# Scattered gate transfers packed into fewer steps, weight loads queued ahead of expert-weight loads, other accumulation banks, a square-root table loaded early

## The chip, the cores and the metric

The kernel runs on one core of one Trainium2 chip. The metric is the time of one execution on the device in microseconds (us); lower is better. The engines are TensorE (PE, matrix products; PEld is its weight load), VectorE (DVE), ScalarE (ACT), GpSimd (POOL), and SyncE (SP), which here only issues transfers. Transfers go over 16 DMA engines.

## What is computed

One decoder layer on 512 tokens of width 2048: a projection, a convolution branch and a differential attention branch, a gated mix, then a layer norm, a product-key mixture of experts ("PEER"), a second layer norm and a gated per-layer embedding. The change lies in the experts' part, and in a helper of the norms:

```python
q = (xb @ w_q).reshape(TOKEN_BLOCK, PEER_HEADS, 2, PEER_HALF)
s = einsum('thcd,hcnd->thcn', q, sub_keys)
vals, idx = lax.top_k(s, PEER_TOPK)            # 8 heads x 16 picks of 128 x 128 experts
...
g = softmax(best)
h = gelu(einsum('td,thkd->thk', xb, u_tab[ids]))
y = einsum('thk,thkd->td', g * h, v_tab[ids])
```

A token has 8 x 16 = 128 picks (head h, pick k; n = 16 h + k in the kernel).

## The kernel before

Every matrix product is made in three matmuls from operands split into a high and a low part (whi, wlo of the weights; ahi, alo of the data), so a block of 8 x 128 x 128 weights costs 24 matmuls. All weights, the two expert tables among them, stream through one buffer of two units (`raw`), a unit being 1 MB or two blocks. SP loads a unit once both low parts of the unit that lay there are made (`load_unit`, L398), ACT makes the high part (`hi_part`, L993) as soon as the block four earlier is done on PE, and the low part is made by POOL (L554) or, from block DVE_LO of the fifth stage on, by DVE (L1520).

**First expert stage** (blocks B5 to B6, 256 blocks in 64 steps of `expert_step`): PE multiplies the inputs of the first 416 tokens with all 16384 rows of `u_tab`; units alternate between PSUM banks 0 and 1. ACT applies gelu and writes the results into `expert_spill` in DRAM (L1182 to L1184, semaphores `gelu_out`, `evac5`). The last 128 tokens are not computed densely: POOL gathers rows of `u_tab` with an indirect DMA, 160 rows in all (`gather_u`, L602; buffer `urows`, four deep, so that row n waits for the use of row n - 4), and DVE takes the dot product of each (`extra_dot` L1532 for the first 32 rows, whose other operand `x1e` is in SBUF; `dot` L1526 for the others, whose other operand `quad` is in PSUM). DVE's order is written out by hand: `expert_tile` (L1559) is one low part, a few gate sums, and in three of four steps one dot; 24 rows go with 32 blocks.

**Gates.** For the first 384 tokens, in three groups a of 128, a dense matrix of gates is needed in DRAM beside the gelus. DVE sums the gates of equal picks (`sum_gate` L1538, `sum_gates` L1554: 384 sums spread over SUM_BLOCKS of the steps), and POOL scatters each column with an indirect DMA, one "put" of 128 words (`put_gate` L572, L580). There are 3 x 128 = 384 puts. `put_gates(n)` (L591) issues those whose entry in PUT_ROW is n just behind the gather of row n, on the same queue. Before the first put of each head but the first (n % 16 == 0), POOL waits until all earlier puts of the same group a have landed (L579). The order is: groups 0 and 1 with heads alternating, 256 puts; then group 2, 128 puts, head after head. The third group's gates need a result of the first 40 rows (`extra_gates`, issued behind row 76; DVE's wait L1548).

**Second expert stage** (from B6, 16 groups of 8 units): for each group DVE forms the products gate x gelu, eight slices (`expert_weights` L1601: three instructions a slice, semaphore `w_ok`), from `hg`, which SP loads from `expert_spill` in pairs of slices into two slots (`load_hg` L473). PE multiplies them with `v_tab` (`value_group` L897; unit u in banks 0,1 if u is even, 2,3 if odd), and DVE adds the results into `res` (L1653). The first product slice k of a group waits for w_ok of that slice. Slices 0 and 1 of the two kinds of `xwhi` and `xwlo` overlay `urows` and `ahi`, so the first group's slices are formed after the last dot, the second's after PE's last block of the first stage (L1630).

**SP's order at the border of the stages** (L480 to L522) is an in-order queue. Behind the load numbered k = 6 of the last twelve of the first stage it waits for all 384 puts (`put`), then loads hg slices 0 to 3. Behind the waits on w_ok that free a slot come the next pairs: ahead of that, or behind it, the loads of the weights.

PE waits for `evac5` of the last unit before it starts the second stage (L915).

**Norms**: `norm_squares` (L1006) squares 8 or 16 slices on ACT for PE to sum and then takes the square root; it is called three times.

Of the kernel before, what the change touches and what calls it, by code (L numbers as in the profile page):

```python
# [18 lines left out]
P = 128  # L19
# [27 lines left out]
U5 = 128  # L47
# [44 lines left out]
PUTS = 3 * NP  # L92
PUT_ROW = [6 + 154 * j // PUTS for j in range(PUTS)]
SUM_BLOCKS = 204

# [10 lines left out]
def build(nc, ws, xT, pT, cpar, pvec, lamT, keysT, u_tab, v_tab, out):  # L106
# [6 lines left out]
    with ExitStack() as ctx:  # L113
# [163 lines left out]
        gone = small("gone", [P, TD // P, NP])  # L277
        same = small("same", [P, 2, NP])
        xsrc = small("xsrc", [P, 2, NP])
# [117 lines left out]
        def _(sp):  # L397
# [82 lines left out]
            for k in range(2 * (64 - POST)):  # L480
                load_unit(B5 // 2 + 2 * POST + k, k % 2)
                if k == 2:
                    sp.dma_start(pin[:], pT).then_inc(p_in, 16)
                if k == 6:

                    for a in range(TD // P):
                        sp.wait_ge(put[a], 16 * NP)

                    for s in range(2):
                        sp.wait_ge(gelu_out[s], 16 * 4)  # L490
                    for s in range(2):
                        load_hg(s, s)
                if k in (9, 10):

                    sp.wait_ge(w_ok, 2 * (k - 7) - 2)
                    load_hg(k - 7, k - 9)

            def group_loads(g, first=False, hg_pairs=4):

                for k in range(8):  # L500
                    if first and k in (0, 2):

                        for s in range(2):
                            sp.wait_ge(gelu_out[s], 16 * (6 if k == 0 else U5 // 2))
                    if first and k == 0:
                        for pair in range(2):

                            sp.wait_ge(w_ok, 6 + 2 * pair)
                            load_hg(4 + pair, pair)
                    load_unit(g * 8 + (B6 // 2 + k), k % 2)  # L510
                    if k % 2 == 1 and k // 2 < hg_pairs:

                        sp.wait_ge(w_ok, g * 8 + (8 + k + 1))
                        load_hg(sp.snap(g * 4 + (6 + k // 2)), k // 2 % 2)
# [18 lines left out]
        def _(pool):  # L533
# [38 lines left out]
            def put_gate(a, n):  # L572

                if n == 0:
                    pool.wait_ge(offs_ok, 1)
                    pool.wait_ge(zero_out, 16 * NK // 4)
                pool.wait_ge(sum_ok, (n // TOPK * 2 + a) * TOPK + n % TOPK + 1 if a < 2 else 2 * NP + n + 1)
                if n % TOPK == 0 and n:
# [12 lines left out]
            def put_gates(n):  # L591

                if n == 3 * NTG + RING:
                    extra_gates()
                for j in range(PUTS):
                    if PUT_ROW[j] == n:
                        if j < 2 * NP:
                            put_gate(j // TOPK % 2, j // (2 * TOPK) * TOPK + j % TOPK)
                        else:
                            put_gate(TU // P, j - 2 * NP)  # L600

# [33 lines left out]
        def _(pe):  # L635
# [261 lines left out]
            def value_group(g, q):  # L897

                for u in range(8):

                    pe.wait_ge(evac6, g * 8 + (u + 1))
                    for half in range(2):
                        b, s = g * 16 + (B6 + 2 * u + half), 2 * (u % 2) + half
                        pe.wait_ge(lo_done, b + 1)
                        for k in range(8):
                            if u == 0 and half == 0:

                                pe.wait_ge(w_ok, g * 8 + (k + 1))
                            t = slice(k * P, (k + 1) * P)
                            mm = three(ps[s][:, 0:TD], whi[:, s, t], wlo[:, s, t],  # L910
                                       xwhi[q][:, k], xwlo[q][:, k], k == 0, k == 7)
                        mm.then_inc(blk_done, 1)


            pe.wait_ge(evac5, 2 + U5)  # L915
            with pe.Fori(0, 8) as i:
# [75 lines left out]
        def _(act):  # L992
# [12 lines left out]

            def norm_squares(i, n, src):  # L1006
                for k in range(n):

# [254 lines left out]
        def _(dve):  # L1263
# [277 lines left out]
            def sum_gate(j):  # L1541

                if j < 2 * NP:
                    a, n = j // TOPK % 2, j // (2 * TOPK) * TOPK + j % TOPK
                else:
                    a, n = TU // P, j - 2 * NP
                if j == 2 * NP:
                    dve.wait_ge(xw_in, 16 * NJ)  # L1548
                here = slice(0, n // TOPK * TOPK + TOPK)
                dve.scalar_tensor_tensor(same[:, j % 2, here], gflat[:, a, here], gflat[:, a, n:n + 1], gone[:, a, here],  # L1550
                                         ALU.is_equal, ALU.mult, accum_out=gval[:, a, n:n + 1]
# [78 lines left out]
            dve.wait_ge(blk_done, B6)  # L1630
            dve.wait_ge(p_in, 16)
            dve.tensor_copy(phi[:], pin[:])
            dve.drain()
            dve.tensor_tensor(plo[:], pin[:], phi[:].bitcast(F32), ALU.subtract).then_inc(p_ok, 1)

            dve.wait_ge(hd_gelu, 1)
            dve.tensor_tensor(hd[:], hd[:], gd[:], ALU.mult)

            def add_values(g, q, first=False, last=False):
                for u in range(8):  # L1640
# [10 lines left out]
                    for n in range(2):  # L1651
                        r = res[:, 2 * u + n, 0:TD]
                        p = ps[2 * (u % 2) + n][:, 0:TD]  # L1653
                        if first:
# [5 lines left out]
                    if last:  # L1660
                        for n in range(2):
# [3 lines left out]
                            else:  # L1665
                                dve.tensor_tensor(msum2[:, 0:TD], msum2[:, 0:TD], res[:, 2 * u + n, 0:TD], ALU.add)
                    if first:
                        for n in range(max(0, 2 * (u - 3)), 2 * (u - 2) if 3 <= u < 7 else 0):
# [93 lines left out]
```

## Time and profile before

| | |
|---|---|
| median of 3 runs | 3819.95 us (3818.35 to 3825.75) |
| the profiled execution | 3826.09 us |
| its span, first to last instruction | 3824.3 us |
| mean granted clock of PE | 0.990 |
| PE busy | 3726.1 us (97%), 19672 matmuls |
| DVE busy | 2615.9 us (68%) |
| ACT busy | 1231.7 us (32%) |
| POOL busy | 1638.9 us (43%) |
| puts, L580 | 384, 446.5 us |

All times in a trace are us from the start of its span. L580 is line 580 of the kernel above; "out<-in" names what an instruction writes and reads; the brackets hold the idle time ahead of an instruction and what ended it; PEclk is the granted share of full clock. The first expert stage runs from about 1450 to 2499, the second from 2505 to 3572. DMA_INDIRECT on POOL is the issue of a gather (L608, L619) or of a put (L580), not the transfer. Some matmul records can be missing from a trace.

### The profile page before, as it was taken

The page shows a single profiled execution, that of the slowest core. Times are in us where ns is not written, and L with a number is a line of the kernel's source. Part 1 is how long each engine was busy: PE and PEld are TensorE (multiplying, and loading weights), DVE is VectorE, ACT ScalarE, POOL GpSimd, SP SyncE. Part 2 cuts the span into 40 slices and gives each one's busy share as a digit, 9 for nine tenths or more (in the row PEclk, how much of TensorE's full clock was granted, in tenths as well). Part 3 has the DMA queues.
Part 4 walks back from the last instruction along what each step waited for, and adds up shares of the span by engine and source line. Part 5 has one row for each costly group of instructions (what it writes and reads, how often), then busy time and mean ns, then how long its engine had stood idle before and what let it go on. Part 6 is the DMA issues. An engine that isn't in the chain of part 4 may idle for free.

```text
span 3824.3 us, 55313 instructions
## 1 busy us (share of the span) xinstructions
PE 3726.1 (97%) x19672; PEld 3394.2 (89%) x19672; DVE 2615.9 (68%) x4104; ACT 1231.7 (32%) x1538; POOL 1638.9 (43%) x1010
## 2 busy tenths in 40 slices
PE   8999999999999999998999999799999999999999
PEld 6888888877887789998999999799999999999777
DVE  3555555553412799877898887678888888888632
ACT  4444444442112423344433332222222222222442
POOL 4444444434444345588777766421212121212233
PEclk9999999999999999999999999899999999999999
DMA  5433443324433123598999989778777777776222
GB/s 186 131 130 130 129 130 130 129 97 140 148 132 115 66 88 137 191 341 319 381 377 376 358 331 333 277 308 319 295 299 296 303 300 300 293 309 259 101 105 80
DMA packets 185328, 848.02 MB, mean 222 GB/s; under 512 B 28912, under 2 KB 70064, under 8 KB 97840
## 3 DMA queue, kind: packets, MB, share of 16 engines
q1 hardware_dynamic: 99760, 507.23, 36.7%
q0 software_dynamic: 54016, 302.28, 20.4%
q10 hardware_dynamic: 31488, 37.76, 2.8%
q8 instruction: 28, 0.46, 0.0%
q14 instruction: 36, 0.29, 0.0%
HBM read 784.02 MB, written 63.11 MB: 222 GB/s over the span
## 4 chain that ended last, share of the span: by engine, by line
PE 75%; DVE 9%; POOL 7%; issue 3%; DMA 3%; ACT 2%; DVEq 1%; ACTq 0%; SPq 0%; POOLq 0%
PE bank L638 24%; PE bank L640 24%; PE bank L639 24%; POOL expert_spill L580 5%; POOL urows L608 2%; DVE hot L1469 1%; DMA raw<-ws 1%; PE quad L681 1%; DMA expert_spill<-gval,goff 1%; DVE sc L1332 1%; PE bank L700 1%; DVE pick L1472 1%; DVE topi L1433 0%; DVE topi L1426 0%; DVE s4b L1427 0%
## 5 line engine op out<-in xcount | busy, mean ns | idle before, releaser
L999 ACT ACTIVATE whi<-raw 128x1024 fp32r<-128x1024 f32 x784 | 822.5, 1059 | 2465.1 <-PE bank L640 1684.3
L638 PE MATMUL bank<-ahi,whi 128*128 128x352 f32 (+1 forms) x3968 | 1431.3, 361 | 66.9 <-DVE wlo L1523 22.0
L640 PE MATMUL bank<-ahi,wlo 128*128 128x352 f32 (+1 forms) x3968 | 1419.1, 358 | 0.0
L639 PE MATMUL bank<-alo,whi 128*128 128x352 f32 (+1 forms) x3968 | 1417.4, 357 | 0.0
L557 POOL TENSOR_TENSOR wlo<-raw,whi 128x1024 fp32r<-128x1024 f32 x316 | 789.5, 2502 | 1054.9 <-ACT whi L999 1026.4
L638 PEld LDWEIGHTS bank<-ahi,whi 128*128 128x128 f32 x3968 | 753.6, 190 | 165.1 <-DVE wlo L1523 46.4
L640 PEld LDWEIGHTS bank<-ahi,wlo 128*128 128x128 f32 x3968 | 751.9, 189 | 77.8
L639 PEld LDWEIGHTS bank<-alo,whi 128*128 128x128 f32 x3968 | 751.3, 189 | 72.5 <-issue 0.5
L638 PE MATMUL bank<-xwhi,whi 128*128 128x384 f32 x2048 | 684.9, 334 | 5.8 <-DVE xwlo L1610 5.8
L640 PE MATMUL bank<-xwhi,wlo 128*128 128x384 f32 x2048 | 684.6, 334 | 0.0
L639 PE MATMUL bank<-xwlo,whi 128*128 128x384 f32 x2048 | 684.6, 334 | 0.0
L1523 DVE TENSOR_TENSOR wlo<-raw,whi 128x1024 fp32r<-128x1024 f32 x472 | 575.1, 1220 | 97.3 <-ACT whi L999 95.0
L619 POOL DMA_INDIRECT vrows<-v_tab,idx x128 | 213.4, 1667 | 871.6 <-DVE yacc L1621 776.5
L580 POOL DMA_INDIRECT expert_spill<-gval,goff x384 | 446.5, 1163 | 156.1 <-issue 119.2
L638 PEld LDWEIGHTS bank<-xwhi,whi 128*128 128x128 f32 x2048 | 385.0, 188 | 6.4 <-issue 6.4
L639 PEld LDWEIGHTS bank<-xwlo,whi 128*128 128x128 f32 x2048 | 385.0, 188 | 0.0
L640 PEld LDWEIGHTS bank<-xwhi,wlo 128*128 128x128 f32 x2048 | 384.9, 188 | 0.0
L1529 DVE SCALAR_TENSOR_TENSOR urows<-urows,quad 128x2048 f32<-128x2048 f32 x128 | 292.2, 2283 | 44.6 <-DMA urows<-u_tab,idx 44.3
L1621 DVE SCALAR_TENSOR_TENSOR yacc<-vrows,hd,yacc 128x2048 f32<-128x2048 f32 x127 | 298.7, 2352 | 24.4 <-issue 21.5
L1332 DVE SCALAR_TENSOR_TENSOR sc<-glu,cur,sc 128x512 f32<-128x512 f32 x232 | 270.1, 1164 | 17.3
L1658 DVE TENSOR_TENSOR res<-res,bank 128x384 f32<-128x384 f32 x240 | 121.9, 549 | 81.0 <-PE bank L640 81.0
L1298 DVE RECIPROCAL rcp<-sums 128x2 f32<-128x2 f32 x32 | 5.3, 166 | 231.2 <-ACTq L1056 231.2
(218 smaller groups left out, 2555.9 us busy)
## 6 DMA issues: line engine op xcount, KB each, us to landing
raw<-ws SPq DMA_DIRECT2D x394, 1024.0 KB
hg<-expert_spill SPq DMA_DIRECT2D x64, 768.0 KB, 7.4
expert_spill<-zero SPq DMA_DIRECT2D x32, 768.0 KB, 7.9
expert_spill<-hst ACTq DMA_DIRECT2D x128, 192.0 KB
gate_spill<-gout ACTq DMA_DIRECT2D x32, 256.0 KB, 2.1
gl<-gate_spill SPq DMA_DIRECT2D x32, 256.0 KB, 2.7
expert_spill<-gval,goff POOLq DMA_INDIRECT x384
xin<-xT SPq DMA_DIRECT2D x8, 512.0 KB, 8.7
```

The source lines that it names most:

```text
L557: nc.gpsimd.tensor_tensor(wlo[:, s], raw[:, s // 2, s % 2], whi[:, s].bitcast(F32), ALU.subtract).then_inc(lo_done, 1)
L580: nc.gpsimd.indirect_dma_start(eg_flat, bass.IndirectOffsetOnAxis(ap=goff[:, a, n:n + 1], axis=0), gval[:, a, n:n + 1], None).then_inc(put ...
L619: nc.gpsimd.indirect_dma_start(vrows[:, n % RING], None, v_tab, bass.IndirectOffsetOnAxis(ap=idx[:, n:n + 1], axis=0)).then_inc(rows_in[n ...
L638: pe.matmul(ps_out, hi, xh, start=first, stop=False)
L639: pe.matmul(ps_out, hi, xl, start=False, stop=False)
L640: return pe.matmul(ps_out, lo, xh, start=False, stop=last)
L999: act.activation(whi[:, s], raw[:, s // 2, s % 2], ACT.Copy).then_inc(hi_done, 1)
L1332: dve.scalar_tensor_tensor(dst, glu[:, w:w + T], cur[:, w:w + 1], acc, ALU.mult, ALU.add)
L1523: dve.tensor_tensor(wlo[:, s], raw[:, s // 2, s % 2], whi[:, s].bitcast(F32), ALU.subtract).then_inc(lo_done, 1)
L1529: dve.scalar_tensor_tensor(urows[:, s], urows[:, s], 1.0, quad[:], ALU.mult, ALU.mult, accum_out=hd[:, bass.ds(n, 1)]).then_inc(rows_used, 1)
L1621: dve.scalar_tensor_tensor(yacc[:], vrows[:, s], w, yacc[:], ALU.mult, ALU.add).then_inc(rows_used, 1)
L1658: ad = dve.tensor_tensor(r, r, p, ALU.add)
```

## The change

1. The 384 puts are spread over rows 6 to 145 instead of 6 to 159, their sums over 184 blocks instead of 204.
2. Their order is a list, PUT_ORDER. Groups 0 and 1 alternate for heads 0 to 6; then come the heads (2,0), (0,7), (2,1), (1,7), and then (2,2) to (2,7). `same` gets a third buffer. The index of the put in the list is what POOL waits for in `sum_ok`.
3. SP: the loads of hg pairs 2 and 3 move from behind k = 9 and 10 to behind k = 10 and 11; in the first group of the second stage the loads of pairs 4 and 5 move from ahead of its first weight load to behind its first and its second.
4. PE: units of the second stage use the other pair of banks (even 2,3; odd 0,1), and the wait for `evac5` moves from ahead of the stage to ahead of unit 1.
5. ACT: `norm_squares` begins with a square root of one column into `std`.
6. DVE: the split of `pin` into phi and plo moves from ahead of the second stage to the end of its first group.

```diff
-PUT_ROW = [6 + 154 * j // PUTS for j in range(PUTS)]
-SUM_BLOCKS = 204
+PUT_ROW = [6 + 140 * j // PUTS for j in range(PUTS)]
+SUM_BLOCKS = 184
+PUT_HEADS = [(a, h) for h in range(7) for a in (0, 1)]
+PUT_HEADS += [(2, 0), (0, 7), (2, 1), (1, 7)] + [(2, h) for h in range(2, 8)]
+PUT_ORDER = [(a, h * TOPK + k) for a, h in PUT_HEADS for k in range(TOPK)]
+FIRST_EXTRA = PUT_ORDER.index((2, 0))
...
-        same = small("same", [P, 2, NP])
+        same = small("same", [P, 3, NP])
...
-                if k in (9, 10):
-                    sp.wait_ge(w_ok, 2 * (k - 7) - 2)
-                    load_hg(k - 7, k - 9)
+                if k in (10, 11):
+                    sp.wait_ge(w_ok, 2 * (k - 8) - 2)
+                    load_hg(k - 8, k - 10)
...
-                    if first and k == 0:
-                        for pair in range(2):
-                            sp.wait_ge(w_ok, 6 + 2 * pair)
-                            load_hg(4 + pair, pair)
                     load_unit(g * 8 + (B6 // 2 + k), k % 2)
+                    if first and k < 2:
+                        sp.wait_ge(w_ok, 6 + 2 * k)
+                        load_hg(4 + k, k)
...
-                pool.wait_ge(sum_ok, (n // TOPK * 2 + a) * TOPK + n % TOPK + 1 if a < 2 else 2 * NP + n + 1)
+                pool.wait_ge(sum_ok, PUT_ORDER.index((a, n)) + 1)
...
-                        if j < 2 * NP:
-                            put_gate(j // TOPK % 2, j // (2 * TOPK) * TOPK + j % TOPK)
-                        else:
-                            put_gate(TU // P, j - 2 * NP)
+                        put_gate(*PUT_ORDER[j])
...
+                        bank = 2 * ((u + 1) % 2) + half
+                        if u == 1 and half == 0:
+                            pe.wait_ge(evac5, 2 + U5)
...
-                            mm = three(ps[s][:, 0:TD], whi[:, s, t], wlo[:, s, t],
+                            mm = three(ps[bank][:, 0:TD], whi[:, s, t], wlo[:, s, t],
...
-            pe.wait_ge(evac5, 2 + U5)
             with pe.Fori(0, 8) as i:
...
             def norm_squares(i, n, src):
+                act.activation(std[:, 0:1], eps[:], ACT.Sqrt)
...
-                if j < 2 * NP:
-                    a, n = j // TOPK % 2, j // (2 * TOPK) * TOPK + j % TOPK
-                else:
-                    a, n = TU // P, j - 2 * NP
-                if j == 2 * NP:
+                a, n = PUT_ORDER[j]
+                if j == FIRST_EXTRA:
                     dve.wait_ge(xw_in, 16 * NJ)
...
-            dve.wait_ge(p_in, 16)
-            dve.tensor_copy(phi[:], pin[:])
-            dve.drain()
-            dve.tensor_tensor(plo[:], pin[:], phi[:].bitcast(F32), ALU.subtract).then_inc(p_ok, 1)
...
-                        p = ps[2 * (u % 2) + n][:, 0:TD]
+                        p = ps[2 * ((u + 1) % 2) + n][:, 0:TD]
...
+                    if first and u == 7:
+                        dve.wait_ge(p_in, 16)
+                        dve.tensor_copy(phi[:], pin[:])
+                        dve.drain()
+                        dve.tensor_tensor(plo[:], pin[:], phi[:].bitcast(F32), ALU.subtract).then_inc(p_ok, 1)
```

## Rows read from the trace of the kernel before

**Rows 1.** Busy time by stretch: PE, PEld, DVE, ACT, POOL, PEclk, DMA share, GB/s

```profile
1600.00:1700.00 100.00, 97.32 (x603) 96.53 (x602) 77.95 (x153) 48.95 (x53) 72.73 (x51) 1.00 0.85 326
1700.00:1800.00 100.00, 88.87 (x523) 86.61 (x522) 70.99 (x137) 40.47 (x44) 81.72 (x61) 0.97 0.89 313
1900.00:2000.00 100.00, 100.00 (x623) 100.00 (x622) 90.95 (x171) 33.72 (x42) 76.14 (x70) 1.00 0.99 379
...
2300.00:2400.00 100.00, 95.05 (x569) 93.92 (x568) 78.85 (x141) 26.33 (x34) 65.38 (x59) 0.97 0.88 325
2400.00:2460.00 60.00, 50.77 (x290) 49.32 (x289) 38.23 (x61) 11.78 (x15) 41.66 (x40) 0.94 0.82 295
```

**Rows 2.** Waits of PE, 2450 to 2520: total us, times, longest us

```profile
PE bank L638 <- ACT hst L1182: 19.1, 1, 19.1
PE bank L638 <- DVE xwlo L1610: 5.8, 1, 5.8
```

**Rows 3.** Busy time by stretch around the border, columns as in rows 1

```profile
2470.00:2480.00 10.00, 5.50 (x25) 5.51 (x26) 6.71 (x5) 4.71 (x6) 0.00 (x0) 0.62 0.53 189
...
2500.00:2510.00 10.00, 4.79 (x19) 4.82 (x20) 9.29 (x15) 2.92 (x5) 4.24 (x4) 0.66 1.00 393
```

**Rows 4.** SP's queue in order of time, start and us of each stretch

```profile
2401.81 28.87 SPq L403 DMA_DIRECT2D raw<-ws  x4
2463.28 0.89 SPq L475 DMA_DIRECT2D hg<-expert_spill  x2
2464.22 13.99 SPq L403 DMA_DIRECT2D raw<-ws  x3
2491.21 0.38 SPq L475 DMA_DIRECT2D hg<-expert_spill  x1
2491.64 0.47 SPq L403 DMA_DIRECT2D raw<-ws  x1
```

**Rows 5.** Timelines of POOL: one group-2 wait, row 145's gather, the last put

```profile
2244.39 0.97 POOL L580 DMA_INDIRECT expert_spill<-gval,goff  x1 [8.93 <-DMA expert_spill<-gval,goff]
...
2378.39 1.17 POOL L608 DMA_INDIRECT urows<-u_tab,idx  x1 [0.30 <-issue]
...
2459.59 0.97 POOL L580 DMA_INDIRECT expert_spill<-gval,goff  x1 [0.30 <-issue]
```

**Rows 6.** Timelines of DVE (L1606, L1610) and ACT (L1182) at the border

```profile
2487.84 0.56 DVE L1606 TENSOR_TENSOR wt<-hg 128x384 f32<-128x384 f32 x1 [0.30 <-issue]
...
2504.26 0.56 DVE L1610 TENSOR_TENSOR xwlo<-wt,xwhi 128x384 fp32r<-128x384 f32 x1
2504.32 0.44 ACT L1182 ACTIVATE hst<-bank 128x352 f32<-128x352 f32 x1
```

**Rows 7.** POOL's busy time with puts (L580) alone, by stretch

```profile
1626.00:1796.00 170.00, 104.11 (x70) 0.98 0.90 327
1796.00:2200.00 404.00, 219.02 (x203) 1.00 0.99 372
```

**Rows 8.** All engines from 1796 to 2200, columns as in rows 1

```profile
1796.00:2200.00 404.00, 401.07 (x2489) 400.78 (x2489) 354.60 (x666) 142.21 (x170) 310.66 (x288) 1.00 0.99 372
```

**Rows 9.** Timelines of DVE (a dot, L1536) and POOL (a put), early

```profile
1752.58 2.29 DVE L1536 SCALAR_TENSOR_TENSOR urows<-urows,x1e 128x2048 f32<-128x2048 f32 x1 [2.41 <-DMA urows<-u_tab,xg]
...
1753.52 2.19 POOL L580 DMA_INDIRECT expert_spill<-gval,goff  x1 [0.30 <-issue]
```

**Rows 10.** Waits of POOL, 2200 to 2460: total us, times, longest us

```profile
POOL expert_spill L580 <- DMA expert_spill<-gval,goff: 26.7, 4, 8.9
POOL expert_spill L580 <- DVE same L1550: 9.9, 3, 6.2
```

**Rows 11.** ACT's timeline in the second and the third norm

```profile
1230.32 1.23 ACT L1013 ACTIVATE sq<-res 128x512 f32<-128x512 f32 x2 [2.51 <-DVE res L1357]
...
1245.16 1.28 ACT L1016 ACT_TABLE_LOAD   x1
...
3597.41 1.18 ACT L1013 ACTIVATE sq<-res 128x512 f32<-128x512 f32 x2
```

More of the change, by code:

```diff
@@ L92 @@
 PUTS = 3 * NP
-PUT_ROW = [6 + 154 * j // PUTS for j in range(PUTS)]
-SUM_BLOCKS = 204
+PUT_ROW = [6 + 140 * j // PUTS for j in range(PUTS)]
[3 more added lines that the diff above has]
+PUT_ORDER = [(a, h * TOPK + k) for a, h in PUT_HEADS for k in range(TOPK)]
+assert sorted(PUT_ORDER) == [(a, n) for a in range(TD // P) for n in range(NP)]
+FIRST_EXTRA = PUT_ORDER.index((2, 0))
 LEAD = 2
@@ L1541, in sum_gate @@
             def sum_gate(j):
-                if j < 2 * NP:
-                    a, n = j // TOPK % 2, j // (2 * TOPK) * TOPK + j % TOPK
-                else:
-                    a, n = TU // P, j - 2 * NP
-                if j == 2 * NP:
+                a, n = PUT_ORDER[j]
+                if j == FIRST_EXTRA:
                     dve.wait_ge(xw_in, 16 * NJ)
                 here = slice(0, n // TOPK * TOPK + TOPK)
-                dve.scalar_tensor_tensor(same[:, j % 2, here], gflat[:, a, here], gflat[:, a, n:n + 1], gone[:, a, here],
+                dve.scalar_tensor_tensor(same[:, j % 3, here], gflat[:, a, here], gflat[:, a, n:n + 1], gone[:, a, here],
                                          ALU.is_equal, ALU.mult, accum_out=gval[:, a, n:n + 1]
```

## The prediction

> **What bounds the kernel.** PE is busy 97% of the span, so only its gaps can be won, and the busy time by stretch shows where they are. A full stretch of 100 us holds 623 matmuls, 0.1605 us each. Between 1600 and 1800 there are 1126 instead of 1246, so 120 are missing: 19 us. Between 2300 and 2400, 54 are missing, 9 us. Between 2400 and 2460, 290 stand where 374 would: 84 missing, 13.5 us, of which some 5 belong to the long wait below, leaving 8.5 [rows 1]. The waits of PE then name two large gaps at the border of the expert stages, 19.1 us and 5.8 us [rows 2].
>
> The reader is to see three things in the queues. SP's queue: four weight loads up to 2430.7, then nothing until 2463.28, when the first hg pairs go out, and the next weight load only at 2464.22 [rows 4]. The last put is issued at 2459.59 [rows 5] and SP waits for its landing ahead of that load; the 19.1 us are this. POOL's queue: in the early stretch the 70 puts take 1.49 us each, in the middle 203 take 1.08 [rows 7]; a gap of 0.30 us stands ahead of each instruction even if nothing is awaited [rows 5]. The early puts are long because they meet the dots of the first 32 rows: a put at 1753.52 lasts 2.19 us, until 0.84 us after the end of a dot that began at 1752.58 [rows 9]. There POOL, not PE, sets the pace: the ring of four rows is used up and DVE waits for rows, with the low parts queued behind it. The 19 us above are this, and the 17.5 us after 2300 too, where every head of group 2 makes POOL wait for its own last puts (8.93 us in one case [rows 5], four such waits 26.7 us in the list and three more of 9.9 us in all put down to the sums [rows 10]).
>
> **The change, part by part.**
>
> (a) *Denser puts, early.* Rows up to 33 had 70 puts; with 140 rows for 384 puts they get 77. Seven more puts on an engine that sets the pace, at 0.98 + 0.30 us, are 9 us on the path. That takes the stretching as something each dot costs POOL once, since dots are not added. If each put paid the mean of its stretch, 1.49 + 0.30, it would be 12.5 us. No gain is possible here; the bounds are 5 (should a little slack be left) and 13. I take 9. The Trainium skill ("SBUF — State Buffer", section "SBUF: two separate sides") calls the port pair that DVE and GpSimd share an exclusive lock, held for a whole instruction, with descriptors of a POOL-issued DMA unable to be written meanwhile. The long put that ends behind its dot agrees; by the strict reading that every put pays the lock the whole change would come out 3.5 us slower than my sum.
>
> (b) *Denser puts, later.* At row 145's gather, 2378.39 [rows 5], the old schedule has issued 350 puts by the end of that row, the new one all 384. Seven of the 34 are counted in (a); the other 27 cost 1.08 + 0.30 us each, 37 us of POOL. What absorbs them: between 1796 and 2200 POOL is busy 310.7 us with 288 instructions, 86 us of gaps with them, so 7 us are idle [rows 8]. In the same stretch it works off the delay of the early one, about 11 us, which will now not be worked off in full and does no harm by itself. The waits for sums (9.9 us in the list, some of it really transfers [rows 10]) shrink by about 3.5 us. The waits of group 2 do not shrink much before row 145: in the new order five heads follow a head of their own group, at rows 117 to 141, which is as many as the old order has there. So 37 - 7 - 11 - 3.5 = 15.5 us more are lost before row 145. Behind it POOL has only gathers left, and the 8.5 us that PE lost after 2400 go away. Sum +7 us. Bounds: 0 (POOL's spare time is larger than I read) and +20 (its instructions are stretched as in the middle and nothing is worked off).
>
> (c) *The wait for the puts.* The last put comes behind row 145: 2378 plus the 16 us of (a) and (b) and its own tail is about 2400, and with a landing of up to 9 us [rows 5] about 2410. SP asks for it behind k = 6, at about 2431 plus 16. The margin is over 30 us, so the wait vanishes: -19.1 us [rows 2]. In the stretch after it 25 matmuls take 5.50 us at a granted clock of 0.62, where 34 would fit: 1.5 us, which the clock falling behind an idle PE cost [rows 3]. Together -20.6. What is late next: two hg pairs, 1.5 MB, now stand right ahead of the weights of k = 7 in SP's queue with PE at full pace; I put +1 us on that, bounds 0 and 4.
>
> (d) *Border.* Two events release PE at 2504.8: the last slice on DVE, 2504.26 + 0.56, and the evacuation of the last unit on ACT, 2504.32 + 0.44 [rows 6]. The second falls away by the other banks and by unit 1's wait. The first moves because weights k = 10 no longer stand behind the wait for w_ok: they went out at 2491.64 just behind the hg pair at 2491.21 [rows 4]; now k = 10 goes as soon as its buffer is free, and DVE is not held between slices by a late high part. The eight slices and the low parts between them take DVE 17.0 us, from 2487.84 to 2504.82 [rows 6]; with the low parts of the first stage running about 10 us ahead of PE, as they do when nothing stalls, most of that lies under PE's last blocks. The last two slices come behind low parts and behind the fourth hg pair, which can go out only once the second slot is free. I leave 2 us of the wait for that. Before it was 5.8 us, and 19 matmuls in 4.79 us at clock 0.66, where 28 would fit, another 1.5 us [rows 2, 3]: -5.3 us. Bounds: -7.3 and 0.
>
> (e) *Table of the square root.* In the second norm ACT is idle 2.51 us ahead of the first square, so the load of 1.28 us moves from the path into that idle time: -1.3. In the third it starts squares directly behind other work at 3597.41, so the load only moves, plus the small instruction: +0.3. In the first nobody waits. [rows 11]
>
> (f) *Nothing*: the third buffer and the list; the split of `pin`, which now follows the first group, where DVE has no row to add and p_ok is read a thousand us later; PE's extra wait per group, always met.
>
> Sum: 9 + 7 - 20.6 + 1 - 5.3 - 1.0 = -9.9 us. The profiled execution took 3826.1, 6 us above the median shown; I take the difference over to the median: 3810.
>
> **The rivals.** *POOL has slack that I don't see*: (a) and (b) give 5, not 16. For it: PE loses nothing from 1900 to 2000. Against: POOL's sum in rows 8 leaves 7 us. Time: 3799. *POOL becomes the bound of the whole stage, and the result is slower*: puts per row rise from 2.49 to 2.74, so POOL needs (2.74 + 1) x 1.38 = 5.16 us a row, and PE's pace is 32 blocks x 24 x 0.1605 / 24 rows = 5.14. With that, nothing that delays POOL is worked off, and rows 34 to 145 lose steadily. It decides from (a) + (b) = 26 us on (where the gains are used up); with 36 it gives 3830. Against it: a mean of 1.38 holds stretches that a busy POOL can have caught by chance; an undisturbed one needs 4.8. *The border keeps its wait*, because the third and fourth hg pair land late behind a 1 MB load that now goes ahead of them: (d) gives 0, 3815. *The wait for the puts stays*, since POOL ends later than 2440: the stall shrinks only in part, about 3825; with 30 us of margin unlikely.
>
> **How the numbers follow.** About 0.2% (7.6 us) is what a measurement of this kernel can tell from no change. Forecast as summed 0.42, slack on POOL 0.22, border keeps its wait 0.14, POOL bounds the stage 0.17, puts still awaited 0.05. The first lies between 3800 and 3818, so part of it counts as no change. Faster 0.58, the same 0.27, slower 0.15. The range takes the first three cases whole and the near half of the fourth: 3792 to 3827; the likeliest one's own is 3800 to 3818.
>
> **What would show it.** (c): no SP gap near 2440, no PE wait over 3 us for hst; the last put near 2400. (a), (b): more PE waits for wlo L1523 between 1640 and 1800, 28 us instead of 19, and around 2250 to 2400; none after the last put. (d): PE's wait ahead of the second stage about 2 us and granted clock 1.00 behind it. (e): the table's load ahead of the first square, the second norm 1.3 us shorter. Wrong would be: POOL never catching up between 1800 and 2200 while PE shows gaps there, or the first stage no longer than before up to row 145.

## The result, and the profile of the changed kernel

Measured: 3849.76 us median (3846.68 to 3854.07, 4 runs) against 3822.85 (3818.35 to 3827.40, 4 runs) of the kernel before beside it, ratio 1.0066 [1.0051, 1.0081]. The change makes the kernel slower by 27 us; the forecast was 3810, range 3792 to 3827. The profiled spans are 3824.3 and 3844.9, so the traces account for 20.6 us.

Where they lie can be read from the starts of the 256 blocks of the first expert stage and the 256 of the second. These are worked out from PE's timeline (the first of a block's 24 matmuls). Undisturbed, a block of the first stage takes 3.867 us (3.84 in some stretches). B6, the border, is block 256. The differences are taken before rounding.

```
block   before   changed   changed - before
   0    1448.3   1448.2    -0.1
  96    1842.4   1851.1    +8.7    dots of the first rows
 224    2337.4   2376.4   +39.0    rows 34 to 137
 248    2447.6   2478.3   +30.7    last puts of before
 250    2474.5   2490.0   +15.5    the stall of k = 7
 256    2505.2   2515.5   +10.3    border
 262    2531.9   2551.2   +19.2    units 0 to 2
 511    3567.8   3587.0   +19.2
```

Two numbers stand out. Between blocks 96 and 224 the kernel before takes 495.0 us, which is 128 x 3.867 and no loss at all; the changed kernel takes 525.3. And what the border gives back, 5.2 us up to block 256, is lost again six blocks later, and 3.7 us more.

Busy time by stretch, changed kernel, columns as in [rows 1]:

```profile
1900.00:2000.00 100.00, 97.58 (x598) 96.77 (x597) 84.88 (x170) 30.50 (x39) 78.51 (x71) 0.98 0.94 346
...
2300.00:2400.00 100.00, 88.01 (x517) 86.27 (x518) 73.73 (x131) 26.04 (x33) 69.29 (x62) 0.97 0.84 305
...
1796.00:2200.00 404.00, 393.07 (x2427) 389.78 (x2426) 342.66 (x676) 132.32 (x163) 316.83 (x291) 1.00 0.96 354
```

The stretch from 1900 to 2000, without a loss before, now lacks 25 matmuls. The last row answers to [rows 8]: POOL is busy 316.83 us with 291 instructions, each with a gap of 0.30 ahead of it, 87.3 us; together 404.1 of 404. POOL has nothing idle left there. The DMA engines did not become the fuller queue: their share falls from 0.99 to 0.96, and what they move from 372 to 354 GB/s. The waits of the same kernel, 1800 to 2470:

```profile
POOL expert_spill L584 <- issue: 89.9, 295, 0.3
DVE urows L1535 <- DMA urows<-u_tab,idx: 87.8, 44, 6.2
```

DVE waits for gathered rows 87.8 us in 44 places (39.3 in 21 before, same view, 1800 to 2440), as POOL, with puts in front of them, issues the gathers late; DVE's low parts stand behind these dots. PE's list, 1800 to 2450, names them:

```profile
PE bank L639 <- DVE wlo L1529: 31.3, 19, 3.2
```

Before it was 12.6 us in 8. The chain of work that ended last (part 4 of the page of the profile) shows the same from the end: of its time PE holds 63% and POOL 13%, before 75% and 7%.

SP's queue of the changed kernel, answering to [rows 4], and PE's waits from 2450 to 2560, answering to [rows 2]:

```profile
2463.90 0.89 SPq L480 DMA_DIRECT2D hg<-expert_spill  x2
2470.51 30.26 SPq L408 DMA_DIRECT2D raw<-ws  x4
...
2518.91 0.33 SPq L408 DMA_DIRECT2D raw<-ws  x1
2519.28 0.43 SPq L480 DMA_DIRECT2D hg<-expert_spill  x1
```

```profile
PE bank L639 <- DVE res L1654: 6.0, 1, 6.0
PE bank L639 <- ACT hst L1188: 4.9, 2, 3.9
PE bank L639 <- DVE xwlo L1613: 1.3, 1, 1.3
```

SP no longer waits for puts: the last one is issued at 2418.88. What is left of the stall is 3.9 us: the weights of k = 7 go out at 2470.51 behind the hg pairs and arrive 17 us later, as ACT's timeline shows:

```profile
2487.53 2.00 ACT L1003 ACTIVATE whi<-raw 128x1024 fp32r<-128x1024 f32 x2 [12.29 <-DMA raw<-ws]
```

The 6.0 us ahead of unit 2 are new. DVE's timeline has their cause, the pair issued at 2519.28 right behind the weights of unit 2:

```profile
2534.39 0.56 DVE L1609 TENSOR_TENSOR wt<-hg 128x384 f32<-128x384 f32 x1 [11.36 <-DMA hg<-expert_spill]
...
2538.78 1.01 DVE L1654 SCALAR_TENSOR_TENSOR res<-res,bank 128x384 f32<-128x384 f32 x2
```

DVE stands 11.36 us at this slice with the evacuation of unit 0 queued behind it, and the banks of unit 0 are those of unit 2. Between 2530 and 2550 the granted clock is 0.74.

### The profile page after: what moved, and what is told of

The parts are those of the page before. It is cut to its first block, busy times and chain, and to the rows that moved or that the text cites. A ratio compares the mean times of both kernels' runs of the same rounds, so it can differ in the third digit from the quotient of the medians.

```text
span 3844.9 us, 55332 instructions
## 1 busy us (share of the span) xinstructions
PE 3732.2 (97%) x19672; PEld 3395.0 (88%) x19672; DVE 2620.2 (68%) x4104; ACT 1227.2 (32%) x1541; POOL 1645.9 (43%) x1010
## 4 chain that ended last, share of the span: by engine, by line
PE 63%; POOL 13%; DVE 11%; issue 5%; DMA 5%; DVEq 1%; ACT 1%; ACTq 0%; SPq 0%; POOLq 0%
PE bank L639 20%; PE bank L641 20%; PE bank L640 20%; POOL expert_spill L584 9%; POOL urows L609 3%; DMA urows<-u_tab,idx 2%; DVE urows L1535 1%; PE quad L682 1%; DMA raw<-ws 1%; DVE hot L1475 1%; DVE wlo L1529 1%; DVE sc L1338 1%; PE bank L701 1%; DMA hg<-expert_spill 1%; DVE pick L1478 1%
## 5 line engine op out<-in xcount | busy, mean ns | idle before, releaser
L1535 DVE SCALAR_TENSOR_TENSOR urows<-urows,quad 128x2048 f32<-128x2048 f32 x128 | 292.4, 2285 | 89.5 <-DMA urows<-u_tab,idx 87.8
L1338 DVE SCALAR_TENSOR_TENSOR sc<-glu,cur,sc 128x512 f32<-128x512 f32 x232 | 270.1, 1164 | 17.3
L609 POOL DMA_INDIRECT urows<-u_tab,idx x128 | 140.9, 1101 | 69.7 <-DVE urows L1535 35.3
```

Of the source, the lines that this page charges most:

```text
L609: nc.gpsimd.indirect_dma_start(urows[:, n % RING], None, u_tab, bass.IndirectOffsetOnAxis(ap=at_col, axis=0)).then_inc(rows_in[n % RING], 16)
L1338: dve.scalar_tensor_tensor(dst, glu[:, w:w + T], cur[:, w:w + 1], acc, ALU.mult, ALU.add)
L1535: dve.scalar_tensor_tensor(urows[:, s], urows[:, s], 1.0, quad[:], ALU.mult, ALU.mult, accum_out=hd[:, bass.ds(n, 1)]).then_inc(rows_used, 1)
```

## The experiments

They ran in five groups, each beside the kernel before. In three of them (e, f and g) the kernel before took 3949 to 3951 us, in two (h and i) 3823, as at the prediction. Ratios compare within a group. The two kinds of chip are taken up at the end.

### The puts and the rest, apart (e1 to e4)

e1 has the change's list, spacing and order alone, e2 all but these:

```diff
-PUT_ROW = [6 + 154 * j // PUTS for j in range(PUTS)]
-SUM_BLOCKS = 204
+PUT_ROW = [6 + 140 * j // PUTS for j in range(PUTS)]
+SUM_BLOCKS = 184
```

e3 has this spacing with the old order, e4 the order (PUT_HEADS) with the old spacing; both have three `same` buffers.

> The kernel before with parts 1 and 2 alone: the 384 puts over rows 6 to 145, their sums over 184 blocks, the mixed order of heads. Theory A (POOL sets the pace of the whole first expert stage once it has 2.74 puts a row): what the trace of the changed kernel shows up to its block 250 and nothing of the border, so 31 us more lost before block 248 and 15 us of them given back by the shorter wait for the puts: +12 to +20 us against the kernel before. Rival B (the puts cost what was forecast and the border costs the rest): about -4 us.

> The kernel before with parts 3 to 6 alone (SP's order, banks, square root, split of pin), puts as before. Theory A: the border wins its 6 us of waiting and loses 6 us to a late hg pair 4 and 3 us to PE's clock behind it, the norms give about 0: -3 to +6 us. Rival B (the border carries the loss): +15 us or more.

> Part 1 alone: puts over rows 6 to 145 and sums over 184 blocks, but in the old order, group 2 last with seven heads that wait for their own. Theory A: the two waits more that the mixed order saves (6 to 9 us each) fall on a POOL that sets the pace, so 8 to 15 us slower than with the mixed order, +20 to +30 us against the kernel before. Rival (the mixed order is what costs, since it moves group 2's sums and puts forward): faster than with the mixed order.

> Part 2 alone: the mixed order of heads, with the puts over rows 6 to 159 and the sums over 204 blocks as before. Theory A: POOL is spared about two waits of 6 to 9 us late in the stage, the last put comes 8 to 15 us earlier, and the 19 us wait of PE shrinks by as much: -8 to -18 us. Rival (POOL's end is set by the rows, not by its waits): no change within 4 us.

Measured, on a 3950 chip: e1 1.0047 [1.0031, 1.0063], e2 1.0008 [0.9989, 1.0027], e3 1.0029 [1.001, 1.0048], e4 0.9970 [0.9948, 0.9992]. The denser spacing is slower, the mixed order alone a little faster, and the border's edits can't be told from nothing. e1 and e2 came as theory A said. e3 (median +15 us) falls short of theory A's range and is not slower than e1, so these runs don't show that the order spares the denser puts anything; e4 (-5 us) lies between its two theories. The sizes are those of a chip on which the long stall for the puts mostly fails to appear (blocks 248 to 250 take 7.7 us in e2 and 9.7 in e4, both with the old spacing; 23.0 in g2 below), so these four say where the loss is and not how large it is on the other.

### Single steps (f1 to f4)

f1 is the changed kernel. f2 is f1 with the fifth and sixth hg pair ahead of the weights again. f3 is the kernel before with SP's wait moved:

```diff
-                if k == 6:
+                if k == 8:
                     for a in range(TD // P):
                         sp.wait_ge(put[a], 16 * NP)
...
-                    for s in range(2):
-                        load_hg(s, s)
+                    load_hg(0, 0)
+                if k == 9:
+                    load_hg(1, 1)
```

f4 joins f3 with the border's edits (less the groups' loads), the table's load in the second norm alone, an order with heads of group 2 still earlier, and only 50 puts up to row 33:

```diff
+PUT_ROW = [6 + 28 * j // 50 if j < 50 else 34 + 126 * (j - 50) // (PUTS - 50) for j in range(PUTS)]
+SUM_BLOCKS = 196
```

> The changed kernel again, beside the kernel before and three variants on one chip, since the first four experiments ran on a chip on which the kernel before takes 3950 us: the reference for the other three. Theory A: slower by 0.4 to 0.8% on either kind of chip.

> The changed kernel with one thing put back: in the first group of the second stage the loads of hg pairs 4 and 5 go ahead of its first weight load again. Theory: pair 4 lands before DVE asks for it, DVE evacuates unit 0 in time, and PE's wait of 6.0 us ahead of unit 2 and the 2.8 us of low clock behind it go: 6 to 10 us faster than the changed kernel. Rival: the weights' first loads are then late instead and PE waits as long for a low part: no change.

> The kernel before with SP's wait for the puts moved from behind load k = 6 to behind k = 8, hg pair 0 there and pair 1 behind k = 9; puts untouched. Theory: the weights of k = 7 and 8 no longer stand behind the last put, so the wait of 19.1 us and the 1.5 us of clock go without any denser puts, -15 to -21 us where the stall is there (traces of 3824 us); on the slower kind of chip, where PE had no such stall, within 5 us. Rival: the hg pairs then come late for DVE and the border's wait grows by the same.

> A version meant to beat both: 50 puts in the first 28 rows instead of 70, the others evenly to row 159, group 2 from the fourteenth head on with four waits for its own head instead of seven, sums over 196 blocks; SP's wait as in f3; hg pairs 2 and 3 behind k = 10 and 11, pairs 4 and 5 ahead of the group's first load; banks and evac5 as changed; the square root only in the second norm. If POOL sets the pace early and late: -20 (stall) -10 (early) -8 (late) -6 (border) -1: 30 to 45 us faster than before. If it doesn't: only the stall and the border, -20 to -27.

Measured, on a 3950 chip: f1 1.0037 [1.0019, 1.0054], f2 1.0075 [1.005, 1.01], f3 0.9985 [0.997, 1.0001], f4 0.9995 [0.9977, 1.0012]. f2 was no better, if anything slower: with the pair early, blocks 258 to 262 still take 24.1 us (f1 24.6). Its timeline of DVE shows what is late in its place, the weights of unit 2 themselves, which ACT can't split sooner:

```profile
2660.05 1.23 DVE L1528 TENSOR_TENSOR wlo<-raw,whi 128x1024 fp32r<-128x1024 f32 x1 [9.84 <-ACT whi L1002]
```

f3 (median 7 us lower, the interval up to 1.0001) can't be told from the kernel before on this kind of chip. f4 missed its theory: it did win early (block 96 at 1847.2, in f3 1867.2) and had given it all back later (block 224 at 2473.8, in f3 2468.0). What takes it back isn't shown: between 1900 and 2450 POOL waits 113.9 us for DVE, so it isn't POOL's queue alone.

### No puts, and four kernels beside it (g1 to g4)

g1 leaves out all puts, so the experts' gates are not scattered, and SP waits for the sums. The expectation calls them 192; they are 384. g2 is the changed kernel with the spacing of before (6 + 154 j / PUTS, SUM_BLOCKS 204), g3 is e4 with the wait of f3, g4 the changed kernel.

```diff
                 for j in range(PUTS):
-                    if PUT_ROW[j] == n:
+                    if False:
...
-                    for a in range(TD // P):
-                        sp.wait_ge(put[a], 16 * NP)
+                    sp.wait_ge(sum_ok, PUTS)
```

> The kernel before without any of its 192 puts (the gates of the experts are not scattered, SyncE waits for the sums on VectorE instead; rows, gathers, dots and sums stay). Theory: POOL's queue (gather and add of a row, plus the puts) sets the pace of rows 30 to 145 and the stall in front of k=7 is the wait for the last put. Then the TensorE gaps of the first expert stage go: block 224 comes within 5 us of 1448.3 + 224 x 3.867 = 2314.5 on a chip where the kernel before takes 3820 (before 2337.4, changed 2376.4), blocks 248 to 250 take 7.7 us (before 26.9), and the whole kernel is 35 to 45 us faster, about 3780. Rival: the rows' work on VectorE and its unit loads set the pace; then block 224 stays near 2337 and only the 19 us stall goes, about 3801. On a chip of the 3950 us kind: theory 3915 to 3930, rival 3950.

> The changed kernel with the spacing of before: the puts reach to row 160 (6 + 154 j / 192, sums to block 204), heads mixed, and all of the border's and norm's edits. Theory (the denser puts are the whole loss, because POOL has no slack from row 30 on): not slower than before; on a 3820 chip 3810 to 3825, on a 3950 chip 3943 to 3952 (the order alone gave 0.997 there, the border's edits alone 1.0008). Rival (the border's edits themselves cost something, as their swapped banks move the wait to unit 2): 5 to 10 us above the kernel with the order alone, that is 3950 to 3956 on a 3950 chip.

> The kernel before with the heads mixed in the puts' order, its spacing kept, SyncE's wait for the puts moved from behind k=6 to behind k=8, with one pair of rows loaded there and one behind k=9. Theory (the stall at k=7 is SyncE waiting for puts ahead of weights that nothing holds): on a 3820 chip 3795 to 3808, as 15 to 21 us of stall go and the order costs nothing; on a 3950 chip 3935 to 3946 (0.9970 and 0.9985 multiplied give 0.9955). Rival (the wait goes elsewhere, to the pairs of rows that arrive late at the border): within 4 us of the kernel before.

> The changed kernel again, as the control beside the other three. On a 3820 chip 1.0066 as in its first measurement; on a 3950 chip 1.004 as in the run before.

Measured, on a 3950 chip: g1 3771.95, 0.9535 [0.9505, 0.9564]; g2 0.9997 [0.9977, 1.0017]; g3 0.9976 [0.9954, 0.9998]; g4 1.0053 [1.0035, 1.0071]. g1 is far below its theory: the puts cost 179 us there. Blocks 64 to 248 take 711.5 us, 3.867 each, and 248 to 250 7.7. Waits of g1, 1800 to 2420:

```profile
POOL urows L607 <- DVE urows L1528: 423.4, 118, 6.7
```

Now POOL waits for DVE at 118 rows, DVE for no row, and PE does not appear in the list. So on this chip every gap of PE from block 64 to 250 needs the puts; dots, low parts and weights' loads by themselves make none. (Blocks 0 to 64, before most of the puts, take 253.8 us in g1 and 253.7 in g2, 6 us over the pace, so those 6 are not theirs.) The forecast counted 19 us early, 17.5 late and the stall, and took the middle as safe. g2 lies in the range of its theory and of its rival, so it doesn't part them on this kind of chip; g3 came 1 us above its range and within the 4 us of its rival.

### Small puts, and the border (h1 to h3)

h1: puts of the first 16 rows of each tile (the other 112 rows' gates are left out); as many instructions, an eighth of the writes.

```diff
-                    eg_flat, bass.IndirectOffsetOnAxis(ap=goff[:, a, n:n + 1], axis=0),
-                    gval[:, a, n:n + 1], None).then_inc(put[a], 16)
+                    eg_flat, bass.IndirectOffsetOnAxis(ap=goff[0:16, a, n:n + 1], axis=0),
+                    gval[0:16, a, n:n + 1], None).then_inc(put[a], 16)
```

h2: the changed kernel with both low parts of unit 0 two places earlier, and the first of unit 1 one:

```diff
-                if k >= 5:
-                    lo_part(B6 + k - 5, k - 5)
-            lo_part(B6 + 3, 3)
+                if k in (3, 4, 6, 7):
+                    s = (3, 4, 6, 7).index(k)
+                    lo_part(B6 + s, s)
```

h3: g3 with the second stage's other banks, the later wait for `evac5`, the later split of P, and h2's edit.

> The kernel before, each of its 384 puts cut from 128 rows to the first 16 (the gates of the other 112 rows of each tile are not scattered): the same number of instructions on POOL and the same waits, an eighth of the small writes. The kernel with no puts took 3772. Theory A (the puts cost by the time of their instructions on POOL's queue): if a put's record stays near 0.98 us, the gap of 0.30 too, the kernel stays within 15 us of before. Theory B (they cost by the writes that they start, 128 of 4 bytes each, which hold up the weights' loads and the reads of the program's own code on a chip of the 3950 kind: TensorE 0.3 to 1.9 us gaps with nothing awaited in every block from row 33 on): most of the 180 us between 3951 and 3772 goes, 3775 to 3810, and the gaps without a releaser with it. On a chip of the 3820 kind A gives 3815 to 3825 and B 3795 to 3805.

> The changed kernel, with VectorE's two low parts of the first unit of the second expert stage ahead of the weights' rows k=4 and k=5 (before them k=0 to 3 and k=4), so that the load of its third unit, which waits for both, is issued 5 to 8 us earlier. Theory (the wait at the third unit, 6.0 us and 2.8 us of lower clock in the changed kernel, is the weights' load issued only at 2518.91, when both low parts are done at 2518.8, and what is queued behind it): block 256 to 262 takes 5 to 9 us less than in the changed kernel (35.7 at 3820, 33 on the 3950 kind), the whole kernel 5 to 8 us less than it: ratio 1.0045 on a 3820 chip, 1.003 on a 3950 chip. Rival (the rows of the weights k=5 to 7 bound the border): block 256 starts 3 to 6 us later, nothing gained.

> What the runs so far found best in one kernel: the spacing of before with the heads mixed, SyncE's wait for the puts behind k=8 with one pair there and one behind k=9, the first unit's other banks and the later split of P, and the low parts early as in the run beside it; the pairs k=9 to 11 and the first group's loads as before. On a 3950 chip 3932 to 3943 (0.9955 to 0.998); on a 3820 chip 3790 to 3805, as the 19 us stall and 4 to 8 us at the border go. If the pairs of rows come late again at the border (20.6 us between blocks 255 and 256 with the order and the split alone), 3946.

Measured, on a 3820 chip: h1 3803.51, 0.9945 [0.9929, 0.9962]; h2 3843.30, 1.0047 [1.003, 1.0064]; h3 3808.93, 0.9959 [0.9945, 0.9973].

h1's time lies in B's range, but it does not part its theories, as A's condition failed: a put's record is shorter too. POOL's busy time with puts alone, 1796 to 2200, is 200.27 us for 200 puts in h1; in [rows 7] it is 219.02 for 203. With 1.00 us in place of 1.08, PE runs without a gap from block 96 to 224 (494.9 us), as in the kernel before, and loses 1.3 us from 224 to 248, where the kernel before loses 17.3; the stall stays, 16.1 us. That the kernel answers to a tenth of a microsecond a put is what a saturated queue would do, but fewer writes may have helped.

h2 did as its theory says: blocks 256 to 262 take 28.8 us (changed 35.7), the kernel 6.5 us less than the changed one's 3849.8, which was measured in another group. The waits of PE, 2480 to 2560, hold no `res` any more; these are all:

```profile
PE bank L639 <- ACT hst L1188: 4.2, 1, 4.2
PE bank L639 <- DVE xwlo L1613: 2.0, 1, 2.0
```

So what held unit 2 was the moment at which its weights can be asked for, and that is when DVE has made both low parts of unit 0, whose buffer they take: their load goes out at 2517.99 in h2, 0.6 us ahead of block 256, and at 2518.91 in the changed kernel, 3.4 us behind it.

h3 beats both kernels, by 14 us and by 41, and is still 4 us above its range.

### Spacing alone and wait alone, on a 3820 chip (i1 to i3)

i1 is h1, i2 is g2 and i3 is f3.

> The kernel before with puts of 16 rows in place of 128, again, for the case that this chip is of the 3950 kind (on a 3820 chip it gave 3803.5, with a put's record at 0.85 in place of 0.98 us and the gates of 112 of the 128 rows of each tile left out). Theory B (the small writes hold up the weights' loads and the program's own code there): 3800 to 3830 on a 3950 chip. Theory A (the instructions' time on POOL, 40 us less in all): 3930 to 3945. On a 3820 chip again 0.9945.

> The changed kernel with the spacing of before (puts to row 160, sums to block 204), everything else as changed: on a 3950 chip it was 0.9997. Theory (the denser puts are what makes the changed kernel slower; the other edits give what the prediction said or less): on a 3820 chip block 224 starts at 2343 to 2348 as in the kernel with all that was best (2343.5), the stall in front of k=7 is gone only in part, and the time is 3805 to 3822, ratio 0.996 to 1.000, that is 28 to 45 us under the changed kernel. Rival (the order or the border's edits make the loss): 3835 or more.

> The kernel before with nothing moved but SyncE's wait for the puts and its two pairs of rows, from behind k=6 to behind k=8 and k=9 (0.9985 on a 3950 chip, where there is no 19 us stall). Theory (the stall at k=7 on a 3820 chip is this wait alone, in front of weights that nothing holds): 19.1 us go at block 249 and 3 to 6 come back at the border, 3803 to 3810, ratio 0.995 to 0.9975. Rival (the stall goes on to the border, since the last put lands when it does): 3818 to 3823.

Measured: i1 0.9956 [0.9939, 0.9973]; i2 3821.23, 0.9993 [0.9983, 1.0004]; i3 3813.32, 0.9974 [0.9963, 0.9984]. i1 repeats h1, on the same kind of chip.

i2 decides the matter: its theory's range held, its rival's (3835 or more) did not. With nothing but the spacing of puts and sums put back, the 28.5 us between 3849.8 and 3821.2 are gone, its block 224 starts at 2338.5, and the stall is back. (The spacing of the puts and that of the sums on DVE weren't parted. Against the sums speaks that DVE stands idle for gathered rows, 87.8 us in the changed kernel, and that g1, with all sums and no puts, has no gap.) PE's waits, 2400 to 2560, in i2:

```profile
PE bank L637 <- ACT hst L1186: 17.2, 1, 17.2
...
PE bank L637 <- DVE res L1652: 5.3, 1, 5.3
```

The denser spacing shortened this stall by 13.5 us (blocks 248 to 250 take 25.2 us in i2, 11.7 in the changed kernel) and paid for it with 39.4 before block 248. The wait for `res` is there too, so it does not come from the puts; blocks 250 to 262 take 60.3 us, in the kernel before 57.4.

i3: blocks 248 to 250 take 7.7 us, so the stall at k = 7 was SP's wait and the pairs behind it, and nothing that the weights need; but at the border PE stands again (2450 to 2560):

```profile
PE bank L639 <- ACT hst L1183: 15.9, 2, 15.1
```

255 to 256 takes 19.1 us (9.9 before). At block 262 i3 is 13.3 us ahead of the kernel before, and 10 in the medians, 3 us short of its range. The same wait, two loads later, costs less, not nothing: the last put decides (2453.7, in the kernel before 2459.6).

## Why the prediction was wrong

**(a)** forecast +9, measured +8.7 at block 96. Right. The strict reading of the Trainium skill's rule ("SBUF — State Buffer", section "SBUF: two separate sides") that I weighed against it, by which every early put pays the lock, gave 12.5: the trace is nearer to one price for each dot. The page ties the descriptors that can't be written to VectorE operations in a two-port mode; that these dots are such operations is not shown here.

**(b)** is the step that failed. Forecast +7 with bounds 0 and +20, measured +22.0 (blocks 96 to 248: 627.2 against 605.2 us). Its second half was right, -8.2 us after block 224 where I had -8.5. Its first half, "37 - 7 - 11 - 3.5 = 15.5", measured +30.2. POOL's time from row 33's gather (1792.4 and 1801.5) to row 145's (2378.4 and 2415.7) is 586.0 us before and 614.2 after, +28.2. The groups of POOL's instructions in these two stretches (busy, mean ns | idle ahead, by releaser), before and changed:

```profile
L580 POOL DMA_INDIRECT expert_spill<-gval,goff x279 | 303.5, 1088 | 113.4 <-issue 87.8 <-DMA expert_spill<-gval,goff 15.4 <-DVE same L1550 10.2
...
L608 POOL DMA_INDIRECT urows<-u_tab,idx x112 | 123.5, 1103 | 43.5 <-issue 34.8 <-DVE urows L1529 8.6
```

```profile
L584 POOL DMA_INDIRECT expert_spill<-gval,goff x307 | 340.9, 1111 | 117.9 <-issue 89.0 <-DMA expert_spill<-gval,goff 25.9 <-DVE same L1553 3.0
...
L609 POOL DMA_INDIRECT urows<-u_tab,idx x112 | 119.2, 1064 | 34.1 <-issue 32.9 <-DVE urows L1535 1.2
```

The cost was set 9 us too low: the puts' records grew by 37.4 us, not by 27 x 1.08 = 29.2, since 28 more fell into the stretch and each grew a little too (1088 to 1111 ns); with 28 gaps of 0.30 that makes 45.8 where I had 37. Three things give back 17.8 us: less idle time ahead of the gathers 9.4 (I had 7), shorter gathers 4.3, and the waits at the heads of group 2 4.1 (I had 3.5 for the sums). The heads were counted rightly, five in this stretch in either kernel. The lists hide it, as before they put only two of the five down to transfers; the timeline of POOL, kernel before, has the other three:

```profile
2206.17 0.98 POOL L580 DMA_INDIRECT expert_spill<-gval,goff  x1 [3.45 <-DVE same L1550]
...
2281.49 0.97 POOL L580 DMA_INDIRECT expert_spill<-gval,goff  x1 [6.18 <-DVE same L1550]
...
2318.38 1.60 POOL L580 DMA_INDIRECT expert_spill<-gval,goff  x1 [4.94 <-issue]
```

With the two others, 8.93 and 6.42, the five come to 29.9 us before; in the changed kernel they are 25.9.

My fourth term, 11 us for a delay that "will now not be worked off in full and does no harm by itself", has nothing in POOL's time to answer to it: a delay that stays takes no work from POOL. It does harm, as the starts of the gathers on POOL's timeline show. This is how far they lie, worked out from them, behind PE's undisturbed pace of 5.156 us a row (32 x 3.867 / 24), counted from row 0, in us:

```
row     before   i2 (old spacing)   changed
  36      13.3         15.0           22.7
 108      -0.7          2.6           31.4
 145      23.3         13.4           60.3
```

With the old spacing POOL catches up 14 and 12.4 us between rows 36 and 108. In the kernel before the waits and longer records of group 2 then put it back by 24.0 us, and PE feels only what goes beyond the room just won: 17.3 us after block 224, with the lag at 29.7 us at row 159 against 14.8 at row 33. With the denser spacing POOL never catches up; it falls back by another 8.7 us, and then the stretch of the same heads, 28.9 us more, finds PE with no room left. So of the difference between the two kernels 22.7 us of lag arise between rows 36 and 108, where POOL waits at no head, and 4.9 behind it.

**The rival** that POOL bounds the whole stage, with 0.17, is what happened in its mechanism: rows 34 to 145 lose steadily. Its size for (a) and (b) together, 36 us, was set and not worked out, and 30.7 were measured; that they are near is luck. Its pace, 5.16 us a row, was too low: rows 36 to 108 take 5.28 each. I argued against it that the mean of 1.38 us "holds stretches that a busy POOL can have caught by chance". A busier POOL caught more of them, not fewer. A margin of 5.14 against 5.16 us a row was read as about even, when with POOL at 98% it meant that no microsecond was to spare. And its time, 3830, was too low since it took the gains of (c) to (e), 25.9 us, as given, where 10.2 came.

**(c)** forecast -20.6 + 1 = -19.6, measured -15.2. The wait for the puts went (last put issued at 2418.9, forecast about 2400), but PE still waits 3.9 us for the weights of k = 7, behind the hg pairs: the upper bound, 4, not the 1 that I took. That the pairs make these 3.9 us is read from the order of the transfers; i3, with the pairs further behind, has no wait there.

**(d)** forecast -5.3, measured +3.7 over blocks 250 to 262. The wait at the border went fully (255 to 256 in 3.9 us), more than forecast, -6.0. What I didn't ask is what is late next: the weights of unit 2 and the pair behind them have a time of their own (2518.91 + 9.0 and 2519.28 + 15.1 us), which does not come forward with PE's start. Six us of wait and the lower clock took all of it back. h2 shows the cause, i2 that it has nothing to do with the puts; f2 shows that the place of the pair alone is not it, on the other kind of chip.

**(e)** forecast -1.0, measured +1.3. In the second norm nothing was won: the square root now waits 1.22 us for PE, so the table's load had lain beside PE's last sum. ACT's timeline, changed kernel, third norm:

```profile
3616.80 1.28 ACT L1012 ACT_TABLE_LOAD   x1
3618.09 0.20 ACT L1012 ACTIVATE std<-eps 128x1 f32<-128x1 f32 x1
3618.20 1.13 ACT L1019 ACTIVATE sq<-res 128x512 f32<-128x512 f32 x2
```

Here the load and the small instruction stand on the path ahead of the squares, 1.4 us, where I gave 0.3.

**Sum**: 8.7 + 22.0 - 15.2 + 3.7 + 1.3 = 20.5, of the 20.6 between the spans. The medians are 27 apart; 6 us of that are not in the two profiled executions, and no cause for them was looked for.

## What to carry to other kernels

When the spare time of a queue that feeds others is a few us in hundreds, price every instruction moved there in full, and let no backlog stand as a credit: the time in which the queue catches up is the room that later waits use. Test the reading with the work taken out, as one such run shows the floor. A wait removed at a border is worth only the time until the next transfer that was issued against the old schedule, so follow each queue two units on. Moving a wait behind transfers that don't need it (i3, h3) was cheaper than making its producer hurry.

## What the runs showed of the hardware

**Two kinds of chip.** The kernel before takes 3823 us on one and 3950 on the other. Without puts it took 3772 on the slower kind, with no gap from block 64 to 250: what makes the stage slow there needs the puts. (No run without puts fell on the faster kind.) It is not POOL's queue alone there. Waits of g4 (the changed kernel, slower kind), 1900 to 2400:

```profile
POOL urows L609 <- DVE urows L1535: 105.7, 19, 8.2
...
PE bank L641 <- issue: 23.9, 39, 1.8
...
```

POOL waits for DVE, and PE has 55 us of gaps in which it waits for nothing that the profile shows (16.2 and 15.3 us on its two other lines); on the other chips such gaps are not in the list. The granted clock is low with them, 0.91 from 2000 to 2200 in g4, where g1 on the same chip has 1.00, and the DMA share is 0.77 where g1 has 0.95. The puts' small writes holding up the program's own code or loads would fit, and was not shown: the run that cuts the writes (h1, i1) fell on the faster kind both times.

**A put's own time.** Its record is 0.97 to 0.99 us with 128 rows and 0.83 to 0.85 with 16, undisturbed: nearly all of it is not the rows.
